# A product-key expert layer: 32 of 256 tokens through gathered expert rows, the rest dense with the weights standing in both expert products

## The reference

```python
q = (t @ w_pq).reshape(n_tok, 8, 2, 128)
sc = einsum('thcd,hckd->thck', q, sub_keys)            # 8 heads, 2 halves, 128 keys
top_s, top_i = top_k(sc, 16)
cand_s = top_s[:, :, 0, :, None] + top_s[:, :, 1, None, :]
best_s, best_j = top_k(cand_s over 256 pairs, 16)      # expert = i * 128 + j
gate = softmax(best_s)
a = gelu(einsum('thkd,td->thk', expert_u[ib], tb))     # 128 experts of 16384 per token
out = einsum('thk,thkd->td', gate * a, expert_v[ib])
```

## Time and profile before

| what | value |
|---|---|
| median of 3 runs | 2278.89 us (2278.63 to 2279.41) |
| the profiled execution | 2278.16 us |
| its span | 2276.2 us |
| busy: TensorE, VectorE, ScalarE, GpSimd | 98%, 67%, 46%, 7% of the span |
| granted TensorE clock | 0.997 of full speed |
| read from HBM | 410.94 MB |

### The profile page before, as it was taken

How to read it: one execution, slowest core, us unless ns; L and a number is a source line. 1 busy time by engine, 2 the same in 40 slices (tenths; PEclk the granted TensorE clock), 3 DMA queues, 4 the chain that set the end, 5 groups by cost and what they waited for, 6 DMA issues and landing times.

```text
span 2276.2 us, 40524 instructions
## 1 busy us (share of the span) xinstructions
PE 2240.5 (98%) x12484; PEld 1957.0 (86%) x12484; DVE 1521.4 (67%) x2471; ACT 1053.1 (46%) x1539; POOL 157.8 (7%) x194
## 2 busy tenths in 40 slices
PE   7999999999999999999999999999999999999997
PEld 6888888889899988888888888888888888888885
DVE  5555566667768888879999998555555555555555
ACT  5444454446455544454444444444444444444443
POOL 0000000000002221121111111000000000000000
PEclk9999999999999999999999999999999999999998
DMA  6655544445564655554454444556555556666664
GB/s 219 232 188 190 177 164 157 150 146 213 183 205 149 204 177 183 180 180 163 160 166 159 164 162 161 192 185 221 193 193 191 193 191 210 194 193 193 193 193 139
DMA packets 114701, 415.73 MB, mean 183 GB/s; under 512 B 12974, under 2 KB 15662, under 8 KB 114022
## 3 DMA queue, kind: packets, MB, share of 16 engines
q1 hardware_dynamic: 114662, 415.23, 54.8%
HBM read 410.94 MB, written 4.24 MB: 182 GB/s over the span
## 4 chain that ended last, share of the span: by engine, by line
PE 97%; DVE 2%; DMA 0%; issue 0%; ACT 0%; DVEq 0%; SPq 0%; ACTq 0%
PE ps L1313 36%; PE ps L1574 30%; PE ps L1320 19%; PE ps L1343 7%; PE ps L1551 3%; PE ps L1418 1%; PE ps L1436 1%; DVE lo L808 1%; PE ps L1427 0%; DMA x_t<-x_t 0%; PE ps L1521 0%; DVE y L1300 0%; PE ps L1510 0%; DMA raw<-w_qk 0%; PE ps L1409 0%
## 5 line engine op out<-in xcount | busy, mean ns | idle before, releaser
L808 DVE TENSOR_TENSOR lo<-raw,hi 128x1024 fp32r<-128x1024 f32 x760 | 933.1, 1228 | 646.9 <-PE ps L1574 335.1
L1313 PE MATMUL ps<-move,hi 128*128 128x512 f32 x3584 | 886.8, 395 | 10.7 <-ACT hi L523 9.9
L523 ACT CAST hi<-raw 128x1024 fp32r<-128x1024 f32 x760 | 791.5, 1047 | 211.8 <-DMA raw<-w_down 110.9
L1313 PEld LDWEIGHTS ps<-move,hi 128*128 128x128 f32 x3584 | 653.8, 189 | 133.4 <-issue 9.9
L1320 PE MATMUL ps<-move,lo 128*128 128x256 f32 x3584 | 490.7, 286 | 5.9 <-DVE lo L808 5.0
L1320 PEld LDWEIGHTS ps<-move,lo 128*128 128x128 f32 x3584 | 467.6, 192 | 30.2 <-DVE lo L808 8.3
L531 ACT COPY upper<-ps 128x256 f32<-128x256 f32 x224 | 83.5, 373 | 582.9 <-PE ps L1313 582.9
L1574 PE MATMUL ps<-hi,act_hi 128*128 128x512 f32 x1024 | 315.5, 389 | 1.6 <-DVE lo L808 1.5
L1574 PE MATMUL ps<-lo,act_hi 128*128 128x512 f32 x1024 | 315.3, 389 | 0.0
L1574 PE MATMUL ps<-hi,act_lo 128*128 128x512 f32 x1024 | 315.2, 389 | 0.0
L1574 PEld LDWEIGHTS ps<-hi,act_hi 128*128 128x128 f32 x1024 | 192.0, 188 | 42.3 <-DVE lo L808 1.9
(11 more groups left out here) (171 smaller groups left out, 1193.5 us busy)
## 6 DMA issues: line engine op xcount, KB each, us to landing
raw<-w_u SPq DMA_DIRECT2D x256, 512.0 KB, 3.3
raw<-w_down SPq DMA_DIRECT2D x256, 512.0 KB, 4.1
raw<-w_qk SPq DMA_DIRECT2D x68, 512.0 KB, 3.3
raw<-w_gate SPq DMA_DIRECT2D x64, 512.0 KB, 3.3
raw<-w_out SPq DMA_DIRECT2D x32, 512.0 KB, 3.3
raw<-w_pq SPq DMA_DIRECT2D x32, 512.0 KB, 3.4
raw<-w_v SPq DMA_DIRECT2D x28, 512.0 KB, 3.3
raw<-w_o SPq DMA_DIRECT2D x24, 512.0 KB, 3.3
```

Source lines behind the costliest of these rows:

```text
L523: nc.scalar.copy(hi[slot][:], raw[slot][:]).then_inc(hi_ready, 1)
L808: nc.vector.tensor_tensor(lo[s % LOS][:], raw[s % RAW][:], hi[s % RAW][:].bitcast(F32), ALU.subtract).then_inc(lo_ready, 1)
L1313: ins = nc.tensor.matmul(ps[bank][:], hi[slot][:, col:col + P], m, start=begins, stop=ends)
```

## The change

- **S = 32 tokens** (the last ones of tile 1) leave the dense products, which now run on TD = 224. For them, with 4 copies of each token over the 128 partitions, each of 32 picks (PICKS) has one expert per partition. GpSimd gathers rows of expert_u by index, 128 x 1024 at a time (half a row), 64 gathers (STEPS), and 64 more for expert_v, through two buffers, `rows0` and `rows1`: gather n is issued when VectorE has done with set n - 2.
- VectorE multiplies a set with h (`dot_of`) and sums along it, one set per two chunks, 34 of them in the last 17 bodies of u and 30 in the first 15 of down. After a gelu and the gates it adds weighted rows of expert_v into `acc` (`rows_at`): 32 in the first half of down from chunk 68 on, one per 13/8 chunks, 32 in the second half, one per 7/2 chunks from chunk 4. Matmuls with `fold` add the four copies up.
- **Down is turned**: the weights stand and act moves, 8 high matmuls of 448 columns and 8 low ones of 224 per chunk. Since output channels now lie on partitions, the stage is run in two halves of 128 chunks, one per 1024 channels, with the banks emptied between them (`keep_tiles`). The tail works on channels by tokens, and the output is turned on the host.
- The **spread** handles 112 pairs of tokens, so 112 chunks, has four banks, makes one_j on GpSimd in one operation with the gates, and no longer starts from ones: ScalarE copies the gates into the part of act whose gelu is not there yet (`keep_gates`), VectorE multiplies the rest (`gated_of`).
- Top-k does tile 1 first; the reduction of a body's picks comes a body later (`reduce_picks`), and the softmax of tile 1 and the indices are made in between.
- x1 goes to DRAM as it is, without being transposed; rows of h for the 32 tokens are turned by 16 transposes.
- GpSimd folds squares of the first half's output (`sq2`) between gathers of the second half.

```diff
-PAIRS = T // 2
+S = 32
+TD = T - S
+COPIES = P // S
+PICKS = PH * TOPK // COPIES
+STEPS = 2 * PICKS
+
+PAIRS = TD // 2
...
+def dots_of(body, s):
+
+    n = 2 * (body - UG) + s // 2
+    return (n,) if s % 2 and 0 <= n < STEPS else ()
+
+
+def adds_of(c, half):
+
+    first, apart = (4, 7 / 2) if half else ((WEIGHED + 2) * BODY, 13 / 8)
+    return tuple(m for m in range(PICKS) if first + int(m * apart) == c)
 
...
+        act_now = [at(f"act_now{i}", (one_at, MOVE + 16 * KB)[i // 2] + i % 2 * 2 * KB, [P, 2 * TD], F32R) for i in range(ACTS)]
...
+                                    xr[:, :, TD:T].unsqueeze(2).to_broadcast([P, KT, COPIES, S]),
+                                    g_ffn[:].unsqueeze(2).unsqueeze(3).to_broadcast([P, KT, COPIES, S]), ALU.mult
+                                    ).then_inc(hs_ready, 1)
+
...
+            def gather(table, n):
+
+                if table == "u_rows" and n >= 2:
+                    pool.wait_ge(dot_done, n - 1)
+                if table == "w_down":
+                    pool.wait_ge(dot_done, min(STEPS, STEPS - 1 + n))
+                    if n >= 2:
+                        pool.wait_ge(row_added, n - 1)
+                lines = A[table].rearrange("c p n -> (c p) n") if table == "w_down" else A[table]
+                nc.gpsimd.indirect_dma_start(rows[n % 2][:], None, lines,
+                                             bass.IndirectOffsetOnAxis(ap=idx[:, n:n + 1], axis=0)
+                                             ).then_inc(row_landed[n % 2], 16)
+            pool.wait_ge(idx_ready, 1)
...
+            for n in range(2, STEPS):
+                gather("u_rows", n)
+            for n in range(PICKS + 2):
+                gather("w_down", n)
+            pool.wait_ge(x2_sq, 2)
+            for n in (4, 2, 1):
+                nc.gpsimd.tensor_tensor(sq2[:, 0:n, :], sq2[:, 0:n, :], sq2[:, n:2 * n, :], ALU.add).then_inc(sq_folded, 1)
+                pool.wait_ge(sq_folded, {4: 1, 2: 2, 1: 3}[n])
+            for n in range(PICKS + 2, STEPS):
+                gather("w_down", n)
...
+            def keep_gates(it, s):
+
+                n = (it - U0) * BODY + s
+                j = blocks_before(n)
+                a.wait_ge(gates_spread, n + 1)
+                nc.scalar.copy(act[:, j:NK, 2 * n:2 * n + 2].rearrange("p j u -> p u j"),
+                               ps[SPREAD_BANKS[s]][:, 0:2 * P].rearrange("p (u j) -> p u j", u=2)[:, :, j:NK]
+                               ).then_inc(g_copied, 1)
+                if s == 0:
+                    gelu_split(it * 2 - 1, 1)
+                if s == 2:
+                    gelu_split(it * 2, 0)
...
+            def kept_tiles(it, s):
+                n = it - HALF - 1
+                if s == 3 and n < 2:
+                    part = slice(4 * n, 4 * n + 4)
+                    nc.scalar.activation(sq2[:, part, :], x2[:, part, :], ACT.Square).then_inc(x2_sq, 1)
+                if s == 3 and n >= 2:
...
+            def reduce_picks(done, row):
+
+                v.wait_ge(picked_row, done)
+                ij = found_ij[:].rearrange("p c t (h k) -> p c (t h) k", k=TOPK)[:, :, bass.ds(row, 1), :]
+                nc.vector.tensor_reduce(ij.rearrange("p c a k -> p c (a k)"), pick_b[:], AX.X, ALU.add).then_inc(best_ready, 1)
...
+            def dot_of(n):
+
+                v.wait_ge(row_landed[n % 2], 16 * (n // 2 + 1))
+                c = n // PICKS * CW
+                nc.vector.tensor_tensor_reduce(rows[n % 2][:], rows[n % 2][:], h_rows[:, c:c + CW], 1.0, 0.0, ALU.mult, ALU.add,
+                                               dots[:, n:n + 1]).then_inc(dot_done, 1)
...
             def gated_of(it, s):
 
-                v.wait_ge(gates_spread, it * BODY + (s + 3))
-                a2 = act[:, :, bass.ds(it * 2 * BODY + 2 * s, 2)].rearrange("p j u -> p u j")
-                nc.vector.tensor_tensor(a2, a2, ps[2 + s % 2][:, 0:2 * P].rearrange("p (u j) -> p u j", u=2), ALU.mult
-                                        ).then_inc(gated, 1)
-
-            def multiplied_of(j, e):
+                n = it * BODY + s
+                j = blocks_before(n)
+                v.wait_ge(g_copied, n + 1)
+                v.wait_ge(act_ready, j)
+                a2 = act[:, 0:j, 2 * n:2 * n + 2].rearrange("p j u -> p u j")
+                nc.vector.tensor_tensor(a2, a2, ps[SPREAD_BANKS[s]][:, 0:2 * P].rearrange("p (u j) -> p u j", u=2)[:, :, 0:j],
+                                        ALU.mult).then_inc(gated, 1)
+
...
+            def multiply_split(it, s):
+                if s % 2:
+                    j, e = it * 2 - (s == 1), 1 if s == 1 else 0
+                    multiplied_of(j, e, 2 * pairs_before(j))
 
             def multiply_u(it, s):
...
+            def act_lo_of(it, s, j):
+
+                v.wait_ge(act_hi_ready, it * BODY + (s + 1))
+                nc.vector.tensor_tensor(act_now[s % ACTS][:, TD:2 * TD], pick1(act, j), act_now[s % ACTS][:, 0:TD].bitcast(F32),
+                                        ALU.subtract).then_inc(act_lo_ready, 1)
...
+            def rows_at(it, s, half):
+                for m in adds_of((it - HALF * half) * BODY + s, half):
+                    n = half * PICKS + m
+                    own = acc[:, half * CW:(half + 1) * CW]
+                    v.wait_ge(row_landed[n % 2], 16 * (PICKS + n // 2 + 1))
+                    if m == 0:
+                        v.wait_ge(w_ready, 1)
+                        nc.vector.tensor_scalar(own, rows[n % 2][:], w_s[:, 0:1], None, ALU.mult).then_inc(row_added, 1)
+                    else:
+                        v.wait_ge(row_added, n)
+                        nc.vector.scalar_tensor_tensor(out=own, in0=rows[n % 2][:], scalar=w_s[:, m:m + 1], in1=own,
+                                                       op0=ALU.mult, op1=ALU.add).then_inc(row_added, 1)
...
+            def down(it, half, last=False):
                 for s in range(BODY):
                     if not (last and s == 3):
                         lo_of(CHUNK0["down"], it, s + 1)
-                    if s % 2 == 0 and not (last and s == 2):
-                        act_lo_of(it * 2 + (s // 2 + 1), (s // 2 + 1) % 2)
-            with v.Fori(0, CHUNKS["down"] // BODY - 1) as it:
-                down(it)
-            down(CHUNKS["down"] // BODY - 1, last=True)
-
-
+                        if not (it == HALF and s == 0):
+                            act_lo_of(it, s + 1, (it - HALF * half) * BODY + s + 1)
+                    if half == 0:
+                        dots_at(CHUNKS["u"] // BODY + it, s)
+                    weights_at(it, s)
+                    rows_at(it, s, half)
+
+            def add_upper(n):
+                v.wait_ge(tile_added, n + 1)
...
+            def highs(s, d, begins=False, ends=False):
+                return nc.tensor.matmul(ps[d][:, 0:2 * TD], hi[s % RAW][:, d * P:(d + 1) * P], act_now[s % ACTS][:], start=begins,
+                                        stop=ends)
+
+            def lows(s, d):
+                return nc.tensor.matmul(ps[d][:, 0:TD], lo[s % LOS][:, d * P:(d + 1) * P], act_now[s % ACTS][:, 0:TD], start=False,
...
+            def down_chunk(it, s):
+
+                high_there(it, s)
+                if s % 2:
+                    low_there(it, s)
+                    for d in range(8):
+                        lows(s, d)
+                    for d in range(8):
+                        ins = highs(s, d)
+                else:
+                    for d in range(8):
+                        highs(s, d)
+                    low_there(it, s)
+                    for d in range(8):
+                        ins = lows(s, d)
+                ins.then_inc(chunk_used, 1)
...
+            def last_body(it, half):
+
+                down_chunk(it, 0)
+                pe.wait_ge(row_added, PICKS * (half + 1))
+                for d in range(8):
+                    nc.tensor.matmul(ps[d][:, 2 * TD:2 * TD + S], acc[:, (8 * half + d) * P:(8 * half + d + 1) * P], fold[:],
+                                     start=False, stop=False, skip_group_check=True)
+                down_chunk(it, 1)
+                high_there(it, 2)
...
-        "w_down": np.ascontiguousarray(f["peer_v"][0].reshape(NK, NK, 2, CW).transpose(1, 2, 0, 3).reshape(-1, P, CW)),
+        "u_rows": np.ascontiguousarray(f["peer_u"][0].reshape(NK, NK, 2, CW).transpose(2, 1, 0, 3).reshape(-1, CW)),
+        "w_down": np.ascontiguousarray(f["peer_v"][0].reshape(NK, NK, 2, CW).transpose(2, 1, 0, 3).reshape(-1, P, CW)),
```

648 lines of the change are left out of this document (414 added, 234 removed).

## The result

| | before | after |
|---|---|---|
| median of the runs | 2278.88 us (4: 2278.63 to 2279.41) | 2217.47 us (4: 2212.93, 2216.0, 2218.95, 2219.18) |
| profiled execution, its span | 2278.16, 2276.2 us | 2212.93, 2211.1 us |

The ratio is 0.9727, interval 0.971 to 0.9744: faster by 61 us. The forecast was 126 us faster, 2153 us with a range from 2135 to 2200. The sign was right, the size was off by half, and the result lies above the range.

The account below looks back on a forecast made before the run. It took TensorE's own stream, busy 98% of the span, to bound the kernel. From 2278.2 us, gains of 147.8 and costs of 22.1 gave 2152.5, forecast as 2153 us, with a range from 2135 to 2200 (chance 0.66).

Parts of the forecast that it names:

- Items 6 and 7: u and down: each dot and each addition takes VectorE 1.28 us, covered by TensorE's work, costed at nothing.
- Rivals A, D and E: A: dots at half rate, 2193, 0.12; D: late gathers make it slower, 2342, 0.04; E: VectorE limits each chunk anyway.
- Rival A: Dots on VectorE at half rate: two chunks take it 5.55 against 4.92 us, +40, 2193 us; chance 0.12.
- The chunk of 2.46 us: u and down: 8 high matmuls at 0.201 and 8 low at 0.1065 us make a plain chunk of 2.460 us.
- Rival C: Dense stages: low matmuls get no shorter with fewer columns, floor at 0.120 us, +55, 2208 us; chance 0.05.
- Item 2: Top-k bodies in u: VectorE takes the bound at 10.2 us a body against TensorE's 9.84; -24.2 us.
- Item 3: Spread in u: a loop through three engines takes 6.0 us per two chunks; 112 chunks gain 26.3 us.
- Items 8 and 9: Transfers at 320 to 344 GB/s with dots and packed additions cost +6 us; gather latency of 5 us is covered.
- item 9: Gather latency taken as 5 us; dots allow 8.5, packed additions 6.2 plus 0.9 of slack, so covered.
- Rival B: Gathers land late, L = 9.0 us: dots +15, packed additions +37, 2202 us; chance 0.13.
- Item 10: Second half of down: GpSimd's folds delay the gather of row set 34, stalling TensorE; +7 us, bounds 4.8 and 14.
- Item 11: Turns and tail: fold matmuls +1.4, squares +1, turn between halves +2, u to down +3, tail +1.7 us.

Follow-up runs that it names:

- experiments 3 and 4: Against the changed kernel: 3, GpSimd's pick product on one of 16 rows, 2196.88 us; 4, VectorE's top-k work spread over a body's four chunks, 2205.46 us.
- experiment 1: The kernel before with narrower dense matmuls in its v, gate, out and u stages, left-out columns not computed: 2200.55 us.
- after_again: The changed kernel itself, unaltered, timed once more beside the mended kernels: 2215.23 us, ratio to before 0.9714.
- experiment 2: The changed kernel without its gathers but the first two and without waits for them, VectorE's work kept: 2189.84 us.
- b_widths: The kernel before with dense matmuls narrowed by stage to low widths of 240, 192, 232 and 224 columns: 2200.55 us.
- a_all_13_again: Changed kernel with gathers ahead of folds, even top-k steps, gates copied first, x1 reload in quarters, additions still at 13/8; timed again: 2185.4 us, ratio to before 0.9574.

## Why the prediction was wrong

**Items 6 and 7, dots and additions on VectorE: right.** 1.30 and 1.28 us, covered in the plain chunks, and without the gathers the packed part loses 0.1 us. Rivals A, D and E fell: a dot is no double pass, the kernel is faster, and plain chunks went from 2.785 and 2.72 us to 2.51. (Rival A's 5.55 us does not follow from its parts, which make 5.8 and some 58 us of loss; nothing else hangs on it.) The Trainium skill, Vector Engine (DVE) Microarchitecture Reference, Points that are easy to get wrong, gives half throughput to the scalar_tensor_tensor form with two sources in SBUF that are not bf16. The trace does not show it: the additions, which are of that form, take 1.280 us for 1024 elements and the low part's plain subtraction 1.22. The dot is recorded as an operation of its own kind (CUSTOM_DVE_ANT_0) and takes 1.220.

**The chunk of 2.46 us was the first failure.** The prediction put a 224-column matmul on the line through 256 and 512 columns ("224 is just outside the low one, but far above") and took "the 0.09 us at which the 128-column matmuls of the spread start" as proof that no floor is near. Four starts have three intervals between them: 0.36 us holds three and the change of form, so the row says 0.11 and a remainder and never 0.09. Taken one by one in the trace of before, they start 0.113, 0.109 and 0.112 us apart there, with a median of 0.111 over the whole spread. It is the floor itself. It costs 0.05 us a chunk: 12.8 us in the down stage, 3.4 in the 68 plain chunks of u, and half or all of 5.6 in the spread, some 20 us. Rival C named it, with 0.120 for 0.111. Each matmul here loads 128 columns of weights first. The Trainium skill, TensorE: Matmul & The Clock Gate, LDWEIGHTS (loading the stationary operand), gives such a load P/1.2 ns, an estimate of 0.107 us for 128 columns. The measured 0.11 is near it, but no run here changes the width of the weights.

**Item 2, top-k: the wrong bound.** I added VectorE's busy time up over a body and found 10.2 us. Both things that it met instead are about place: one step had more than its share ahead of the low part that TensorE waits for, and GpSimd's product lengthens what runs beside it. Of the 17 us missed here, experiments 3 and 4 gave back 9.9 and 9.8 us. TensorE's own time for a body is 10.04 us with the floor, so the 0.4 to 0.6 us that both variants stay above it is still order and waiting; it was not taken apart further. The Trainium skill, SBUF — State Buffer, Who interferes with whom, says that a VectorE instruction with two inputs in SBUF contends with a GpSimd instruction that reads SBUF, and calls the port pair that they share an exclusive lock. The trace agrees: the low part starts at 862.70, the product, which started first, ends at 863.63, and the low part ends 1.08 us behind that, nearly its whole 1.22.

**Item 3, the spread: right in kind.** The loop gives 6.1 us per two chunks where 6.0 was forecast (it grew from 3.00 to 3.10 a chunk in the course of the stage). 5.8 us missed. Widths alone would have given nearly the same (experiment 1), so the new work here cost little, and the 10.4 us of the loop were there to be had.

**Items 8 and 9, transfers: the rate right, the latency and the cost too low.** Demand and supply were read correctly (344 GB/s forecast, 340 GB/s at a share of 0.90, and it can be carried). The step that failed is item 9's "I take 5 ... Covered": it was read from dense loads at 193 GB/s, and under the full queues gathers took 8.0 us in the median for the dots and 7.2 for the packed additions (after_again), whose own limit in item 9 was 6.2. The cost was then priced as an average, 0.07 us a chunk. Where two buffers are all that lies between a full queue and an engine that works in order, lateness comes in stops of whole microseconds: 16.3 us in the profiled execution, 3.7 to 20.4 over thirteen. Behind some of the stops the clock falls as well: in the profiled execution behind 2 of its 6. Rival B had this place and nearly this latency (9.0) with a larger price (37 us); for the dots its latency came too, but their 8.5 us of cover held (3.5 us of waits). That gathers cause it is shown by experiment 2, and that the late ones stand at the stops by their times. What starts a series of slow gathers was not found: neither the pace (13/8 to 15/8) nor the session nor the kernel decides it alone, and a third row buffer, which would give each gather more time, was not tried. That a stop makes the next gathers slow, since the loads catch up behind it (377 GB/s in the window after the stop shown), would fit, but is not shown.

**Item 10, the fold stall: right in place and chain, 10.7 for 7.** L was 4.2 us (1892.14 to 1896.38), the folds 4.9, so the terms of 5 and 5 were a little too large. What made it longer are two that the sum lacked: VectorE's 2.56 us beside the folds (3.2 us of the loss stay without gathers) and the clock.

**Item 11.** The tail took 15.2 us and 15.3 were forecast. The turn of the halves with the fold matmuls cost 4.6 for 3.4, the start of the down stage 4.3 for 3, the last four chunks 5.6 for 1, which was not taken apart.

In sum, the 61 us that were missed are: the floor some 20, top-k 17, transfers 11, the fold stall 4, and 9 of small terms (the query stage, the turns, the last chunks). So the miss has several causes and not one.

## What to carry to other kernels

Before a stream of matmuls is narrowed, measure the start-to-start time at the narrowest size that the trace holds, and count intervals, not starts; here nothing was gained below 240 columns. When work is added beside a bound engine, look at each step and not at the sum: what stands in order ahead of the operation that the bound engine waits for, and what the neighbour engine does to it meanwhile. Take the latency of a transfer from rows with the load that it will meet, not from quieter ones. A cover with a few per cent of room on queues with two buffers behind them should be priced in whole stops, as a range.

## What the runs showed of the hardware

- Matmuls of 128x128 weights, each with weights of its own, start every 0.111 to 0.112 us from 192 to 240 columns (b_widths) and also at 128 and at 32 (the spread and the fold matmuls of the changed kernel), every 0.120 at 256, 0.174 at 384, 0.203 at 448, 0.227 at 512.
- Beside a GpSimd instruction that reads SBUF, VectorE's two-input operations took 2.01 instead of 1.22 us, 1.22 instead of 0.41, and 2.56 instead of 0.39.
- After 6.4 us without work TensorE's granted clock was 0.50 (1.2 GHz) for the next 4 us. After 2.2 us it was 0.81 and 0.76 in the mean of two such windows in one place; behind stops of 1.5 us (changed kernel, 1701 us) it stayed at full speed.
- An indirect gather of 128 rows of 4 KB holds GpSimd for 1.67 us (expert_u) or 1.20 us (expert_v). It landed 5.9 to 10.7 us after its start beside the dots (median 8.0), 5.0 to 8.7 in the packed part (7.2) and 4.3 to 5.6 beside the sparse additions (5.2), all in after_again; in a_all_13_again the packed part's median was 5.2.
